# A two-layer hybrid trunk: first half banks of two hidden tiles ahead of a chunk, one operand split moved to even banks, one small matmul moved by nine

## What is computed

```
x = x + mixer(rmsnorm(x))          layer 0: forgetting attention, layer 1: three dilated groups
x = x + square(relu(rmsnorm(x) @ w1)) @ w2        w1: 1024 x 4096, w2: 4096 x 1024
```

## Time and profile before

| | |
|---|---|
| median of three runs | 1634.73 us |
| profiled execution, its own time | 1632.28 us |
| its span | 1630.4 us |
| PE busy | 1564.7 us (96%), 8674 matmuls |
| DVE busy | 997.2 us (61%) |
| ACT busy | 652.7 us (40%) |
| POOL busy | 445.0 us (27%) |
| PE's share of the chain that ended last | 79% |
| the eight MLP chunks | some 83 us each |

### The profile page before, as it was taken

The page is one execution under the profiler, slowest core; times in us unless marked ns, Lnnn a source line. Parts: engine busy times, 40 slices in busy tenths (PEclk is TensorE's granted clock), DMA queues, the critical chain, the costliest instruction groups (busy, mean ns, idle before and its releaser), DMA issues.

```text
span 1630.4 us, 23551 instructions
## 1 busy us (share of the span) xinstructions
PE 1564.7 (96%) x8674; PEld 1296.3 (80%) x8674; DVE 997.2 (61%) x1708; ACT 652.7 (40%) x1084; POOL 445.0 (27%) x608
## 2 busy tenths in 40 slices
PE   7999988999999999899999999999998999999998
PEld 6776655877878787799998888998766778787877
DVE  4466565557575858643647576555655466676759
ACT  5433332344343535434435334443442343444433
POOL 3412100020111621172527465443822110101110
PEclk9999999999999999899999999999999999999999
DMA  6211100456565664322222412222232467475653
GB/s 171 83 61 40 64 28 1 155 129 166 144 152 150 143 161 90 119 88 78 65 79 77 131 54 64 78 78 65 66 106 91 122 154 203 103 190 119 177 130 81
DMA packets 111355, 173.49 MB, mean 106 GB/s; under 512 B 13216, under 2 KB 45984, under 8 KB 111008
## 3 DMA queue, kind: packets, MB, share of 16 engines
q1 hardware_dynamic: 91664, 134.51, 26.6%
q0 software_dynamic: 17408, 33.56, 12.5%
q10 hardware_dynamic: 2192, 4.20, 0.7%
HBM read 165.89 MB, written 6.36 MB: 106 GB/s over the span
## 4 chain that ended last, share of the span: by engine, by line
PE 79%; DVE 8%; POOL 4%; issue 3%; ACT 3%; DMA 1%; SPq 1%; DVEq 0%; ACTq 0%; POOLq 0%
PE ps L562 52%; PE ps L834 16%; PE ps L620 3%; PE ps L652 2%; PE ps L634 2%; POOL qrs L1641 2%; PE ps L664 2%; PE ps L593 1%; DMA raw<-in_mlp_w 1%; DVE pT_sb L1309 1%; POOL qss L1640 1%; DVE w_l L1442 1%; ACT w_h L908 1%; ACT p_sb L975 1%; DVE qss L1220 1%
## 5 line engine op out<-in xcount | busy, mean ns | idle before, releaser
L562 PE MATMUL ps<-w_h,act_h 128*128 128x512 f32 x768 | 316.8, 412 | 7.7 <-DVE w_l L1187 3.4
L562 PE MATMUL ps<-w_h,act_l 128*128 128x512 f32 x768 | 306.6, 399 | 0.0
L562 PE MATMUL ps<-w_l,act_h 128*128 128x512 f32 x768 | 305.6, 398 | 0.0
L562 PEld LDWEIGHTS ps<-w_h,act_h 128*128 128x128 f32 x768 | 191.7, 250 | 26.9 <-issue 10.5
L562 PEld LDWEIGHTS ps<-w_l,act_h 128*128 128x128 f32 x768 | 191.8, 250 | 15.9
L562 PEld LDWEIGHTS ps<-w_h,act_l 128*128 128x128 f32 x768 | 192.6, 251 | 14.2
L562 PE MATMUL ps<-act_h,w_h 128*128 128x512 f32 x512 | 200.0, 391 | 3.9 <-DVE act_l L1203 3.4
L562 PE MATMUL ps<-act_l,w_h 128*128 128x512 f32 x512 | 199.3, 389 | 0.0
L562 PE MATMUL ps<-act_h,w_l 128*128 128x512 f32 x512 | 199.2, 389 | 0.0
L975 ACT ACTIVATE p_sb<-ps,negmax 128x128 f32<-128x128 f32 (+3 forms) x256 | 93.4, 426 | 262.5 <-DVE negmax L1268 191.7
L834 PE MATMUL ps<-w_h,op_h 128*128 128x512 f32 x448 | 176.6, 394 | 10.4 <-DVE op_l L1469 10.4
(11 more groups left out here) (195 smaller groups left out, 2663.2 us busy)
## 6 DMA issues: line engine op xcount, KB each, us to landing
w_raw<-in_dil_w_in SPq DMA_DIRECT2D x72, 512.0 KB, 3.8
raw<-in_mlp_w SPq DMA_DIRECT2D x64, 512.0 KB, 5.0
raw<-in_mlp_w POOLq DMA_DIRECT2D x48, 512.0 KB, 6.1
w_raw<-in_mlp_w SPq DMA_DIRECT2D x32, 512.0 KB, 4.8
w_raw<-in_fox_w_in SPq DMA_DIRECT2D x22, 512.0 KB, 3.6
p_sb<-in_mlp_w SPq DMA_DIRECT2D x16, 512.0 KB, 5.3
pT_sb<-in_mlp_w SPq DMA_DIRECT2D x16, 512.0 KB, 6.4
w_raw<-in_mlp_w POOLq DMA_DIRECT2D x16, 512.0 KB, 8.3
```

Of the source, the lines that this page charges most:

```text
L562: return mm(ps_out, lhs[i], rhs[j], start=(k == 0 and term == 0), stop=(k == KT - 1 and term == 2))
```

## The change

It has four parts. (1) `a11_high` and `a11_low` of k are issued at the end of the turn of the even bank 2k, behind the weight splits of that turn, in place of the turn of bank 2k+1. (2) The half banks run ahead at a chunk's end, and at an MLP's start, are those of tiles 0 and 1, 24 matmuls where there were 12; the following chunk starts with the second halves of both. (3) The wait of tile 1 is accordingly that of a bank last read by product 5's second add. (4) The matmul of the turned norms stands before the first matmul of b = 1, where it stood before k = 5 of b = 0.

```diff
--- before.py
+++ after.py
@@ -715,11 +715,11 @@
                                 prepare(3, 1, 3)
                             if k == KT // 2:
                                 prepared(3, 1, 3)
-                            if k == 5:
-
-                                pe.wait_ge(quad_done, 1)
-                                pe.wait_ge(spread_done, 1)
-                                mm(ps_s[0][:, 0:NT], spread, place[:, :], start=True, stop=True).then_inc(turned_full, 1)
+                        if proj == 2 and b == 1 and k == 0 and term == 0:
+
+                            pe.wait_ge(quad_done, 1)
+                            pe.wait_ge(spread_done, 1)
+                            mm(ps_s[0][:, 0:NT], spread, place[:, :], start=True, stop=True).then_inc(turned_full, 1)
                         last = token_bank(B, k, term, b % 4, 0 if kind == "fox" else LAYOUT[kind])
                         if k == KT - 1 and term == 2:
                             last.then_inc(proj_full, 1)
@@ -791,8 +791,8 @@
                 def hidden(i, b, k):
 
                     if k == 0 and b < 2:
-                        if isinstance(i, int) and i == 0 or b == 1:
-                            pe.wait_ge(x_added, i * ADDS + (x0 - 1 + b))
+                        if isinstance(i, int) and i == 0:
+                            pe.wait_ge(x_added, x0 - 1 + b)
                         else:
                             pe.wait_ge(x_added, (i - 1) * ADDS + (x0 + 2 * S4_B22 + b + 1))
                     elif k == 0:
@@ -836,7 +836,7 @@
 
                 def chunk(i, final):
                     for b in range(KT):
-                        for k in range(KT // 2 if b == 0 else 0, KT):
+                        for k in range(KT // 2 if b < 2 else 0, KT):
                             hidden(i, b, k)
                     for q in range(PRODUCTS):
                         seventh(i, q, 0)
@@ -848,15 +848,17 @@
                             for t, half in PREP_AFTER_MLP[2 * (q - S3_T3):2 * (q - S3_T3) + 2]:
                                 prepare(3, half, t)
                     if not final:
-                        for k in range(KT // 2):
-                            hidden(i + 1, 0, k)
+                        for b in range(2):
+                            for k in range(KT // 2):
+                                hidden(i + 1, b, k)
 
 
                 prepared(n, 0, NT - 1)
-                for k in range(KT // 2):
-                    if k == 2:
-                        prepare(n, 1, NT - 1)
-                    hidden(0, 0, k)
+                for b in range(2):
+                    for k in range(KT // 2):
+                        if b == 0 and k == 2:
+                            prepare(n, 1, NT - 1)
+                        hidden(0, b, k)
                 prepared(n, 1, NT - 1)
                 with pe.Fori(0, CHUNKS - 1) as i:
                     chunk(i, False)
@@ -1087,15 +1089,15 @@
                             w1_high(layer, i, 3)
                         act.wait_ge(proj_full, mlp_unit(layer, i, b) + 1)
                         fn(qn[:, b % 2, :], ps_proj[b % 2][:, :], ACT.Relu).then_inc(relu_done, 1)
-                        if b % 2 == 1:
-                            a11_high(i, b // 2)
-                        elif b:
+                        if b and b % 2 == 0:
                             s12_high(i, b // 2 - 1)
                         if b in (1, 3):
                             w1_high(layer, i, b + 3)
                             w1_high(layer, i, b + 4)
                         if b >= 3:
                             w2_high(i, (b - 3) // 2, (b - 3) % 2)
+                        if b % 2 == 0:
+                            a11_high(i, b // 2)
                     s12_high(i, KH - 1)
                     w2_high(i, S2_T2, 1)
                     for q in range(1, PRODUCTS):
@@ -1533,7 +1535,6 @@
                         square(i, b)
                         if b % 2 == 1:
                             sums(i, b // 2)
-                            a11_low(i, b // 2)
                         elif b:
                             s12_low(i, b // 2 - 1)
                         if b in (1, 3):
@@ -1541,6 +1542,8 @@
                             w1_low(layer, i, b + 4)
                         if b >= 3:
                             w2_low(i, (b - 3) // 2, (b - 3) % 2)
+                        if b % 2 == 0:
+                            a11_low(i, b // 2)
                     s12_low(i, KH - 1)
                     w2_low(i, S2_T2, 1)
                     add(i, 0, 0, final)
```

## The result

The changed kernel takes 1625.18 us (median of four runs, 1622.42 to 1626.72) against 1634.6 us for the kernel before (four runs, 1633.3 to 1635.1). The ratio is 0.9942, with a 95% interval of 0.9924 to 0.9959. That is 9.4 us less, where 9.7 were forecast.

A forecast was written before the change was run, and what follows sets the result against it. TensorE, busy 96% of the span, was taken as the bound, its idle time as winnable. 9.5 + 0.3 + 0 + 1.6 - 1.7 = 9.7 us off the median 1634.73 gave 1625.0 us, range 1620.5 to 1629.5.

The forecast's parts named there:

- The a11 split: Product 0 in chunks 0 to 2 of both layers: TensorE's stall for a11 goes, 1.6 us a chunk, 9.5 us.
- late next: Nine matmuls into product 1: TensorE next needs the last split of s1 and s2, ready at least 2.5 us early.
- The last chunks: Last chunk of each layer: VectorE is the bound, so only 0.3 us in layer 1 and 0 in layer 0.
- The half banks: MLP starts: waits for `act_l` are filled but return as waits for bank 0's square, 2.1 to 2.6 us each; gain 0.
- the clock: Behind the longer pauses at the two MLP starts: clock falls to 1.2 GHz, 1.7 us each; one charged, -1.7 us.
- the case "both": The clock falls behind both MLP starts: -3.4 us, result 1626.7 us; chance 0.24.
- The turned norms: The turned norms' matmul, moved nine matmuls later, no longer waits for POOL's operand: 1.6 us, between 1.3 and 1.8.
- new wait at product 1: Rival: a late DMA delays the s1 and s2 split, TensorE stops nine matmuls into product 1; 1629.8 us, chance 0.06.
- in the loop at tile 2: Bank 0 is full only 2.7 us before tile 2 needs it; relu to square takes 1.3 us, so cost 0.
- late DMA at the a11 split: Rival: a11 split, behind bank 6's weight split, waits for a late DMA; slower, 1639.7 us, chance 0.02.

The follow-up runs named there:

- halves_only: The kernel before with parts 2 and 3 alone (two half banks ahead): 1635.28 us, ratio 1.0006.
- late_waits: The full change with VectorE's waits for cleared accumulators and roots moved from the MLP's start to just before its first add: 1616.81 us, ratio 0.9896.
- no_halves: The full change without parts 2 and 3 (one half bank ahead as before): 1623.45 us, ratio 0.993.
- turned_only: The kernel before with part 4 alone (the turned norms' matmul nine matmuls later): 1632.82 us, ratio 0.9991.
- a11_only: The kernel before with part 1 alone (a11 split at even banks on ScalarE and VectorE): 1624.17 us, ratio 0.9939.

## Why the prediction was right

**The a11 split, 9.5 us.** The mechanism and the size held. A middle chunk went from 83.20 to 81.60 us, the restart behind the stall included. Part 1 alone took 5.0 and 5.1 us off the two MLP stages, and the forecast was 4.8 and 5.1. In the change the three stalls of each layer's first chunks account for 4.8 us twice, 9.6 in all. What was named as late next, the last split of s1 and s2, has 2.8 us to spare (7.5 less 4.7), against at least 2.5 forecast.

**The last chunks, 0.3 us.** Right in that they win next to nothing. Undoing the edit there cost 0.3 us in layer 0, where 0 was taken and the stretch itself varies by 1 us from kernel to kernel, and 0.2 to 0.8 in layer 1, where 0.3 was. The place was wrong in one respect. I wrote that the wait of 3.76 us for `act_l` in layer 0 would grow by 1.6. It stayed at 3.77. VectorE's lateness shows at TensorE's transposes before it instead, 1.21 us at 648.58. A wait of this kind (1.2 to 1.7 us) stands there in all six kernels without the a11 stall in the last chunk, and in none of the four with it is it over 0.4. Where the rest of the 1.6 us went is open: the pause at the entry to the dilated block is 0.4 us longer, but it also moves by over 1 us with the clock. Whoever runs ahead of a busy engine meets it at the first thing that is asked of it, not at the largest wait of the old trace.

**The half banks, 0, and the clock, -1.7.** The `act_l` waits went and came back as waits for the square, of 2.40 and 2.13 us, within the 2.1 to 2.6 forecast. The clock fell behind both in the profiled execution, so of this execution the case "both" (-3.4) is the one to compare: forecast 8.0, measured 8.7 from the common point on. Over the executions profiled with such a pause it fell behind four of six; behind the ten pauses of 1.6 to 1.8 us at the same place in the other kernels, never. To count one of two was fair, by these six a little low. The cost of a fall, read as 1.7, is 1.6 by the MLP starts. The Trainium skill (TensorE: Matmul & The Clock Gate, Part 1: The HAM clock gate) says that the monitor runs free of the kernel. The runs agree: a pause of 2.40 us was followed by 0.51 in the full change, and one of 2.39 by 1.00 in halves_only.

**The turned norms, 1.6 us.** Right in size: 1.3 to 2.2 us by the kernels whose clock did the same, 2.0 between before and the change. The 0.28 us at the query turn went as well, and I had given a part of it back to the small matmul, which did not take it.

**The sum.** From the common point on the change is 8.7 us shorter: 9.6 for the stalls in the first three chunks, nothing to speak of in the last ones (0.2 us more in layer 0, 0.3 less in layer 1), 2.3 in the dilated block, less 3.2 for two falls of the clock. The forecast for two falls was 8.0. The terms hold one by one, to 0.3 us for the stalls and the last chunks and to 0.7 for the dilated block. By the medians it is 9.4 against 9.7. That the median met the forecast to 0.2 us is better than its terms deserve, since four executions of the change differ by 4 us among themselves, and how often the clock falls in them was a guess.

**The rivals.** No new wait at product 1, none in the loop at tile 2, no late DMA at the a11 split. What the prediction did not see is that the new wait could be removed: it called the half banks worth nothing, which is true only as long as VectorE waits for POOL at the head of the MLP.

## What to carry to other kernels

A split that needs one bank only should not stand in an engine's queue behind work that needs the next bank. Find the last operand that the consumer waits for, and see what is queued ahead of it for no reason of data. When a wait is filled with other work and comes back unshortened one step later, the next thing to look at is what the second waiter waits for: here a wait for cleared accumulators stood half a chunk ahead of their first use, and moving it or the clearing turned a neutral edit into one worth some 4 us. An engine that is made faster in the last stage, where another is the bound, wins a few tenths at most, so count such stages out of the sum.

## What the runs showed of the hardware

**A little over 2 us of TensorE's idle time can cost 1.6 us more.** At the MLP starts pauses of 2.1 to 2.4 us were followed by some 3.4 us at a granted clock of 0.5 (1.2 GHz) in four cases of six, and pauses of 1.6 to 1.8 us in none of ten. Each fall costs 1.6 us, so joining two short pauses into one long one can lose time though the total pause is the same: halves_only has 2.39 and 2.13 us in one piece each, where before had 1.8 and 1.6 with 0.2 and 0.3 later. These are counts at one place and no bound for others. In late_waits a pause of 1.53 us in the dilated block (970.57) was followed by 0.50 from 972.26 on, while the kernel before, with the same pause at 980.68, stayed at 1.00.

**Two executions can be 5 us apart before the first changed instruction, and the clock has a large share in it.** The point at 323.7 us before lay between 323.08 and 328.20 in ten profiles. The clock had been down for 6.8 us before it in late_waits (323.08) and no_halves (323.45), for 10.2 in before (323.70), and for 20.5 in turned_only, the latest. Whole executions go the same way: of a11_only's five the shortest, 1620.53 us, shows a mean granted clock of 0.995 and the longest, 1626.41, one of 0.990. A single profile's span should be compared from a common point on, not as a whole, and medians of four or five such executions do not settle 1 or 2 us.

**A small operation on POOL took six times as long beside VectorE's split.** The 128x4 operation of line 1632 took 1.19 and 1.15 us in late_waits, where a split of 128x1024 ran on VectorE at the same time (from 330.00 in layer 0), and 0.20 us in all eighteen other cases. POOL's four clearings (3.63 us) and the split beside them (1.22) kept their times. No run here shows why.
